# Output part of the state-space layer: the sums of squares and their root stand ahead of the second late modulation group on TensorE and ACT, not behind it

## The reference, cut to what matters

```
y_mb = (y_mb + mb_d[:, None] * xm).reshape(b, t, MB_DIM) * silu(zg)
y_mb = y_mb.reshape(b, t, MB_GROUPS, MB_DIM // MB_GROUPS)
y_mb = y_mb * rsqrt(mean(y_mb * y_mb, -1) + NORM_EPS) * mb_norm_w
```

```
m_lat = split(c_lat_act @ w_ada[i] + b_ada[i], 6)
m_ctx = split(c_ctx_act @ w_ada[i] + b_ada[i], 6)
```

## Time and profile before

| What | Value |
|---|---|
| median of three runs | 3778.58 us |
| the profiled execution's own time | 3774.8 us |
| its span, first to last instruction | 3773.0 us |
| PE busy | 3460.4 us (92%) |
| DVE busy | 2537.6 us (67%) |
| ACT busy | 1889.9 us (50%) |
| POOL busy | 149.7 us (4%) |
| mean granted TensorE clock | 0.951 of full speed |

### The profile page before, as it was taken

The page is one execution under the profiler, slowest core; times in us unless marked ns, Lnnn a source line. Parts: engine busy times, 40 slices in busy tenths (PEclk is TensorE's granted clock), DMA queues, the critical chain, the costliest instruction groups (busy, mean ns, idle before and its releaser), DMA issues.

```text
span 3773.0 us, 70951 instructions
## 1 busy us (share of the span) xinstructions
PE 3460.4 (92%) x27016; PEld 3020.6 (80%) x27016; DVE 2537.6 (67%) x3378; ACT 1889.9 (50%) x2511; POOL 149.7 (4%) x161
## 2 busy tenths in 40 slices
PE   6966696879999999899999999999999999999899
PEld 4854383768989885788888888888899899998898
DVE  2456657555555627689999999999656655557555
ACT  3222222123344424478888888888544644444643
POOL 0068000000000000000000000000000000000000
PEclk8977797989999999899999999999999999999999
DMA  5222303003545530289999999999454355554354
GB/s 199 92 93 95 135 3 142 7 19 124 182 154 181 183 117 12 100 327 362 363 359 364 362 360 363 361 362 362 157 181 159 108 166 181 164 181 149 96 189 156
DMA packets 199350, 723.28 MB, mean 192 GB/s; under 512 B 21888, under 2 KB 25472, under 8 KB 198784
## 3 DMA queue, kind: packets, MB, share of 16 engines
q1 hardware_dynamic: 198576, 714.01, 53.7%
q0 software_dynamic: 592, 6.69, 0.4%
HBM read 719.57 MB, written 1.05 MB: 191 GB/s over the span
## 4 chain that ended last, share of the span: by engine, by line
PE 83%; DVE 6%; POOL 4%; ACT 3%; DMA 2%; issue 1%; SPq 1%; DVEq 0%; ACTq 0%; POOLq 0%
PE ps L305 23%; PE ps L306 23%; PE ps L307 23%; PE ps L657 1%; DMA ada_late<-wada 1%; PE ps L1432 1%; PE ps L525 1%; POOL ptmp L1207 1%; PE ps L1429 1%; POOL ptmp L1210 1%; PE ps L1699 1%; POOL ptmp L1208 1%; PE ps L1716 1%; PE ps L1423 1%; PE ps L2032 1%
## 5 line engine op out<-in xcount | busy, mean ns | idle before, releaser
L268 DVE TENSOR_TENSOR w_lo<-w_raw,w_hi 128x1024 fp32r<-128x1024 f32 x529 | 647.2, 1225 | 751.9 <-ACT w_hi L264 748.9
L264 ACT ACTIVATE w_hi<-w_raw 128x1024 fp32r<-128x1024 f32 x529 | 558.7, 1058 | 800.4 <-PE ps L307 741.4
L305 PE MATMUL ps<-a_hi,w_hi 128*128 128x256 f32 (+1 forms) x3000 | 895.8, 299 | 66.6 <-DVE a_lo L552 24.5
L2117 DVE TENSOR_TENSOR mlo<-mraw,mhi 128x1024 fp32r<-128x1024 f32 x726 | 877.1, 1224 | 91.9 <-ACT mhi L2113 62.8
L306 PE MATMUL ps<-a_lo,w_hi 128*128 128x256 f32 (+1 forms) x3000 | 897.1, 299 | 0.0
L307 PE MATMUL ps<-a_hi,w_lo 128*128 128x256 f32 (+1 forms) x3000 | 894.2, 298 | 0.0
L2113 ACT ACTIVATE mhi<-mraw 128x1024 fp32r<-128x1024 f32 x726 | 770.5, 1062 | 180.3 <-PE ps L307 149.1
L305 PEld LDWEIGHTS ps<-a_hi,w_hi 128*128 128x128 f32 x3000 | 578.3, 193 | 92.5 <-issue 51.4
L306 PEld LDWEIGHTS ps<-a_lo,w_hi 128*128 128x128 f32 x3000 | 572.3, 191 | 16.1 <-issue 0.5
L307 PEld LDWEIGHTS ps<-a_hi,w_lo 128*128 128x128 f32 x3000 | 572.5, 191 | 15.8
L305 PE MATMUL ps<-mhi,x_hi 128*128 128x512 f32 x968 | 395.5, 409 | 1.9 <-DVE mlo L2117 1.9
(11 more groups left out here) (495 smaller groups left out, 4642.4 us busy)
## 6 DMA issues: line engine op xcount, KB each, us to landing
mraw<-wexp SPq DMA_DIRECT2D x726, 512.0 KB, 5.3
w_raw<-wstream SPq DMA_DIRECT2D x529, 512.0 KB, 3.3
ada_late<-wada SPq DMA_DIRECT2D x80, 512.0 KB, 4.8
ada_raw<-wada SPq DMA_DIRECT2D x16, 512.0 KB, 9.1
bia<-bias POOLq DMA_DIRECT2D x1, 4096.0 KB, 14.2
con<-consts SPq DMA_DIRECT2D x1, 1824.0 KB, 16.1
conb<-constsb POOLq DMA_DIRECT2D x1, 1224.0 KB, 7.6
hT<-ctxT SPq DMA_DIRECT2D x1, 1024.0 KB, 12.4
```

The source lines that it names most:

```text
L264: nc.scalar.activation(whi[:, slot, :], raw[:, slot, :], ACT.Copy).then_inc(hi_ready.sem, 1)
L268: nc.vector.tensor_tensor(wlo[:, slot, :], raw[:, slot, :], whi[:, slot, :].bitcast(F32), ALU.subtract).then_inc(lo_ready.sem, 1)
L305: nc.tensor.matmul(out, lhs[0], rhs[0], start=start, stop=False, skip_group_check=skip)
L2117: nc.vector.tensor_tensor(mlo[:, slot, :], mraw[:, rslot, :], mhi[:, slot, :].bitcast(F32), ALU.subtract).then_inc(lo_ready.sem, 1)
```

## The change

Two calls are moved by one place each. On PE the rows of group 1 stand behind the sums of squares, on ACT the copy of those rows stands behind the root.

```diff
         def pe_mbout(pe):
             pe_late_cols(pe, 0, 6)
-            pe_late_rows(pe, 1, 0)
             pe.wait_ge(*S("mb_sq").next("pe"))
             for g in range(2):
                 for i in range(2):
                     last = nc.tensor.matmul(ps[:, 2 + g, :], ones[:], zg[:, 2 * g + i, :],
                                             start=(i == 0), stop=(i == 1))
             last.then_inc(*S("mb_ss").one)
+            pe_late_rows(pe, 1, 0)
             pe_late_cols(pe, 1, 6)
             pe_late_rows(pe, 2, 4)
 
         def act_mbout(act):
             act_late_cols(act, 0)
-            act_late_rows(act, 1)
             act.wait_ge(*S("mb_ms").next("act"))
             nc.scalar.activation(zg[:, 0:2, :], zg[:, 0:2, :], ACT.Sqrt).then_inc(*S("mb_rt").one)
+            act_late_rows(act, 1)
             act_late_cols(act, 1)
             act_late_rows(act, 2)
```

## The result

| | median | runs | from, to |
|---|---|---|---|
| kernel before | 3781.6 us | 16 | 3778.12, 3785.3 |
| changed kernel | 3788.2 us | 16 | 3783.39, 3796.3 |

The ratio is 1.0018, with a 95% interval of 1.001 to 1.0026: the change costs 6.6 us, and the interval excludes no change, though it includes 0.2%. The prediction was +6.7 us and 3785.3 us, with 3788.6 us as the top of its range. The kernel before, too, has a median 3 us above the 3778.58 us that the forecast started from, since those were three runs, and low ones. So it is the difference that the forecast can be held against; the time itself, 3788.2 us, lies close under the top of the range.

What follows compares the result with a forecast made beforehand. The chain, mostly TensorE work, was bound here by GpSimd's `pool_shift` and the load `gup`. Rows 2 end 16.5 us later, idle time takes 9.75, leaving 6.7: 3778.58 + 6.7 = 3785.3 us, range 3780.5 to 3788.6.

Steps and rivals of the forecast that it cites:

- Nothing is taken away: Sums and root around DVE's squares: sums already start 0.11 us after their input, so moving them gains 0.
- What is queued behind the sums: On PE, group 1's quads, tile waits, columns 1, rows 2 and columns 2 queue up; `lora_up` comes 6.7 us later.
- The 1.2 us for `lora` and `gup`: Before quad 5 on PE: GpSimd's two loads lengthen the 4.88 us tile wait by an estimated 1.2 us.
- The reckoning by bytes: At quad 5's tiles, with DMA engines full: 0.52 MB more at 378 GB/s costs up to 1.4 us.
- Everything behind `lora_up` passes the shift on: From `lora_up` to the program's end: no slack behind it, so the whole 6.7 us stay.
- Of those 9.75 are taken up by the idle time that PE had in front of `gup`: On PE before columns 2: idle time absorbs 9.75 us of the 16.5 us delay of rows 2.
- The shift of 16.5 us: On PE, the end of rows 2 moves from 362.4 to 378.9, 16.5 us later.
- The clock did not rise too late: Rival at quad 2 on PE: clock still low, 3.64 us for 1.92, +8.4 in all; chance 0.32 with similar costs.
- Table loads: Rival on ACT before tanh and sigmoid: engine drains before each load, 1.28 us more each, +9.3 in all; chance 0.02.
- The group was not covered: Rival before `gup` on PE: shorter tile waits and free loads let idle time cover the group, +1.3 left; chance 0.06.
- a gain in the rest of the program: Rival in the solve steps: a shift avoids clock drops worth 8.5 us, giving -1.8 in all; chance 0.04.

Runs made afterwards that it cites:

- PE's part alone: Changed kernel with ACT's old order (copy of group 1's rows, then the root), only PE's rows moved behind the sums; ratio 1.0016 to the kernel before.
- the ten repeats: Kernel before with columns 1 computed eleven times in place of once, ten of no use; ratio 1.0074.
- ACT's part alone: Kernel before with only ACT's order changed, the root ahead of the copy of group 1's rows; ratio 1.0016.
- one repeat of the columns: Kernel before with columns 1 computed twice, one repeat of no use; ratio 1.0005.
- the split: Changed kernel with the first quad of group 1 put back ahead of the sums, the second behind them; ratio 1.0009 to the kernel before.
- `gup` later: Changed kernel with GpSimd issuing the load `gup` only after quad 5 has ended, on its own semaphore; ratio 1.0018 to the kernel before.
- the split with the hold: One quad of group 1 ahead of the sums, one behind; SP asks for tile 26 onward only once `lora` and `gup` have landed; ratio 1.0006.
- one repeat with the hold: Kernel before with columns 1 computed twice; SP asks for tile 26 onward only once `lora` and `gup` have landed; ratio 0.9999.

## Why the prediction was right, and where it was not

**Nothing is taken away: right.** The sums start 0.12 us behind their input, the root 7.7 us behind the sums, in both kernels. PE's part alone, with the root 11 us later, cost no more than the whole change, so there was nothing to gain from the root's place.

**What is queued behind the sums: right, with one term mis-sized.** Quad 2 at 1.92 us behind the sums, 4.89 us of wait before quad 3 (4.90 forecast), columns 1 at 3.58 us (3.57), 6.08 us before quad 5 (4.88 + 1.2). Only quad 4's tiles were mis-sized: 5.32 us after quad 3's end (362.95 to 368.27) in place of 4.88. Columns 2 ran at the higher clock (1.92 us for 3.51), and as said ahead, this did not help, since ACT's table loads, tanh and sigmoid ended later still. The 0.44 us of quad 4's tiles are most of what separates 7.2 in the trace from the 6.7 forecast; why these tiles took longer no run shows. The 1.2 us for `lora` and `gup` in the way of quad 5's tiles agree with 6.08 against the 4.85 of PE's part alone. The reckoning by bytes behind them (0.52 MB at 378 GB/s) is not borne out: with `lora` alone in the way the wait was still 5.80 us, and not half way.

**Everything behind `lora_up` passes the shift on: right.** 63.64 against 63.62 us to line 1364. From there to the end the profiled executions differ by up to 12 us, with no relation to what was changed, so they cannot tell. The medians can: +6.6 us in the runs against +7.3 at line 1364, and over all experiments the two agree within 2.1 us, but for the ten repeats (+31.3 against +28.0).

**"Of those 9.75 are taken up by the idle time that PE had in front of `gup`": right for this change, wrong as a rule.** I took the landing of `gup` as a fixed point. It is not: SP's requests for tiles hang on PE's quads, and a delay of quad 5 pushes 2 MB into the moment when GpSimd asks for `lora` and `gup`. ACT's part alone lost 4.1 us to that, one repeat of the columns 2.1 us, both with 8 us of idle time still in front of `gup`. In the changed kernel `gup` was late as well (6.0 us), but it landed at 372.41 + 6.0 = 378.4, 4.4 us ahead of PE's columns 2 at 382.8. The shift of 16.5 us was simply larger than the trap. That this step came out is luck: for delays of 4.3 to 7.1 us the same working fails. Against the start of the sums, one repeat delayed the end of rows 2 by 4.3 us, the split by 7.0 and ACT's part by 7.1; my working says 0 for each of these, and the traces show 2.1, 3.9 and 4.1 us.

**The rivals.** The clock did not rise too late: quad 2 took 1.92 us. In every kernel where the sums stood behind the long pause, that was so. Table loads cost 1.28 us each with the next instruction 0.02 us behind, as in the rows of before; no drain appears. The page ScalarE: Activation LUTs of the Trainium skill (What ACT_TABLE_LOAD costs) gives about 2.66 us for a switch; here tanh starts 1.32 us behind the end of the copy (382.72 to 384.04). The group was not covered, and of a gain in the rest of the program the medians show nothing beyond their noise. The page DMA: Bandwidth & Descriptors of the Trainium skill (Rules for kernel authors) advises to ask early and wait late; the trace agrees, as the wait of 4.9 us stands uncovered in front of quad 3 once the quads have left the time beside DVE's products.

## What to carry to other kernels

Idle time in front of a transfer is slack only if nothing that the delayed engine triggers uses the same DMA engines in that time: here 4.3 us of delay, with 9.75 us of idle time in front, cost 2.1 us. Before counting on it, ask which requests its work releases and when they would fall. And an independent filler in a wait earns its place by what is queued behind it: moving the waiting work ahead of the filler gains nothing when its input comes later anyway, and moving more filler into the idle time gained 0.25% here.

## What the runs showed that I had not expected

The time from line 1364 to the end differs between profiled executions by some 12 us, without regard to what was changed: 3332.6 us before, 3344.6 in the changed kernel, 3344.8 with `gup` later, 3344.7 for the split with the hold, but 3335.7 for one repeat with the hold. A part of it is TensorE's clock falling in places where it stays up in other executions. In the second stack's mixer, 25 us around the same place in the kernel before and in the changed kernel (length, busy us of PE, PEld, DVE, ACT, POOL, then the granted clock):

```profile
3495.00:3520.00 25.00, 21.10 (x144) 18.84 (x144) 15.16 (x19) 17.31 (x22) 0.00 (x0) 1.00 0.27 85
```

```profile
3515.00:3540.00 25.00, 24.37 (x134) 21.36 (x133) 11.08 (x14) 15.43 (x18) 0.00 (x0) 0.78 0.20 64
```

The clock stood at its higher level all along in the one and was at the lower level for nearly half of the other. From the first matmul of line 2369 here to the first of line 2381 it is 7.8 us in the kernel before (3497.40 to 3505.20) and 13.7 in the changed one (3512.96 to 3526.63). It is 13.7 also in the other two executions with 3344.7 and 3344.8 us, and 7.8 with PE's or ACT's part of the change alone, so this place makes 5.9 of the 12 us. Why it falls there in one execution and not in another stays open. This is why the medians of 16 runs are needed for an effect of 6.6 us, and why distances within the trace say it more sharply.
